# Two transformer blocks on one core: window-attention logits computed two heads at a time, and another order of work between the mixer and the experts

## The reference, cut to what matters

```
# first block: sliding-window attention, 8 query heads on 2 key/value heads, with sinks
s = einsum(q, k) * 64**-0.5 + bias            # per head: 64-wide dot products, 128-query blocks, 256-key band
p = softmax(concat([masked s, sink]))[..., :-1];  o = p @ v
# second block, behind the mixer
x  = x + merged @ w_out
h2 = x * rsqrt(mean(x*x) + eps) * norm2_g
g_logits = h2 @ w_router_group + b_rg;   e_logits = h2 @ w_router_expert[group] + b_re
group = argmax(g_logits);   two best experts of the 8 in the group, softmax over the two
y = sum over the two of  gate * ((silu(h2 @ w_gate[e]) * (h2 @ w_up[e])) @ w_down[e])
out = rmsnorm(x + y)
```

## Time and profile before

| | us |
|---|---|
| median of 3 runs | 730.55 (730.4 to 730.85) |
| the profiled execution's own time | 730.1 |
| its span, from the first to the last instruction | 728.2 |
| TensorE busy | 670.5 (92%) |
| VectorE busy | 333.3 (46%) |
| ScalarE busy | 302.5 (42%) |
| GpSimd busy | 78.5 (11%) |

### The profile page before, as it was taken

One profiled execution on the slowest core, in us unless ns is written; L12 is line 12 of the kernel. 1 busy time (PEld: TensorE's weight loads), 2 busy tenths in 40 slices (PEclk: granted clock), 3 DMA queues, 4 the chain that ended last, 5 costly groups with the idle time before them and its releaser, 6 DMA issues.

```text
span 728.2 us, 11450 instructions
## 1 busy us (share of the span) xinstructions
PE 670.5 (92%) x4599; PEld 514.4 (71%) x4599; DVE 333.3 (46%) x576; ACT 302.5 (42%) x512; POOL 78.5 (11%) x58
## 2 busy tenths in 40 slices
PE   6999999899999999998999999998999996768774
PEld 5887865699999999976988999975644442323222
DVE  3145442755566666577553564666632221212113
ACT  3235353554554454455563453334333332222223
POOL 0000000132333333321013000000000000000000
PEclk9999999999999999999999999999999999999998
DMA  8942133354554555542443349557899999999994
GB/s 343 424 181 85 58 116 116 119 190 164 194 201 173 177 194 200 180 174 79 154 174 116 116 174 365 213 198 318 357 422 422 419 422 421 421 421 420 421 421 203
DMA packets 25390, 181.41 MB, mean 249 GB/s; under 512 B 2816, under 2 KB 3072, under 8 KB 3840
## 3 DMA queue, kind: packets, MB, share of 16 engines
q1 hardware_dynamic: 25200, 180.69, 63.8%
q10 hardware_dynamic: 144, 0.07, 0.1%
HBM read 179.70 MB, written 1.05 MB: 248 GB/s over the span
## 4 chain that ended last, share of the span: by engine, by line
PE 71%; DMA 16%; DVE 7%; ACT 4%; issue 1%; POOL 1%; ACTq 0%; SPq 0%; DVEq 0%; POOLq 0%
PE psum L910 39%; DMA more_units<-units_in 7%; PE psum L603 4%; PE psum L1147 4%; DMA early_unit<-units_in 4%; DMA X<-units_in 4%; PE psum L701 3%; PE psum L1171 3%; PE psum L611 3%; PE psum L1163 3%; PE psum L1154 2%; DVE ffn_w_low L474 2%; PE psum L660 2%; ACT ffn_w_high L469 1%; DVE arena L2029 1%
## 5 line engine op out<-in xcount | busy, mean ns | idle before, releaser
L474 DVE TENSOR_TENSOR ffn_w_low<-ring,ffn_w_high 128x2048 fp32r<-128x2048 f32 x57 | 134.6, 2362 | 119.1 <-ACT ffn_w_high L469 119.0
L469 ACT ACTIVATE ffn_w_high<-ring 128x2048 fp32r<-128x2048 f32 x56 | 107.2, 1914 | 144.1 <-PE psum L910 143.8
L910 PE MATMUL psum<-ht_high,ffn_w_high 128*128 128x256 f32 x576 | 163.8, 284 | 1.8 <-DVE ffn_w_low L474 1.1
L910 PE MATMUL psum<-ht_low,ffn_w_high 128*128 128x256 f32 x576 | 163.0, 283 | 0.0
L910 PE MATMUL psum<-ht_high,ffn_w_low 128*128 128x256 f32 x576 | 163.0, 283 | 0.0
L910 PEld LDWEIGHTS psum<-ht_high,ffn_w_high 128*128 128x128 f32 x576 | 110.5, 192 | 3.5 <-issue 1.6
L910 PEld LDWEIGHTS psum<-ht_low,ffn_w_high 128*128 128x128 f32 x576 | 110.5, 192 | 0.3
L910 PEld LDWEIGHTS psum<-ht_high,ffn_w_low 128*128 128x128 f32 x576 | 110.5, 192 | 0.0
L2342 DVE SCALAR_TENSOR_TENSOR weighted<-psum,arena,weighted 128x512 fp32r<-128x512 f32 x31 | 23.3, 751 | 119.4 <-ACT weighted L1669 119.4
L1365 ACT ACTIVATE arena<-psum 128x512 f32<-128x512 f32 (+6 forms) x65 | 34.5, 538 | 87.5 <-PE psum L1147 64.7
L1751 POOL TENSOR_TENSOR rstd<-ms,neghalf 128x1 f32<-128x1 f32 (+3 forms) x19 | 13.3, 698 | 480.1 <-DVE ms L1805 342.0
(11 more groups left out here) (346 smaller groups left out, 1022.1 us busy)
## 6 DMA issues: line engine op xcount, KB each, us to landing
ring<-units_in SPq DMA_DIRECT2D x99, 1024.0 KB, 4.8
more_units<-units_in SPq DMA_DIRECT2D x34, 1024.0 KB, 26.3
small_units<-units_in SPq DMA_DIRECT2D x10, 1024.0 KB, 25.5
early_unit<-units_in SPq DMA_DIRECT2D x5, 1024.0 KB, 26.2
HN<-units_in SPq DMA_DIRECT2D x5, 1024.0 KB, 26.5
features_unit<-units_in SPq DMA_DIRECT2D x4, 1024.0 KB, 24.6
X<-units_in SPq DMA_DIRECT2D x4, 1024.0 KB, 25.0
rows<-units_in SPq DMA_DIRECT2D x4, 1024.0 KB, 26.0
```

Source lines behind the costliest of these rows:

```text
L469: nc.scalar.activation(parts_slot(n)[0], w, ACT.Copy).then_inc(hi_ready, 1)
L474: nc.vector.tensor_tensor(l, ring[:, n % RING, :], h.bitcast(fp32), SUB).then_inc(lo_ready, 1)
L910: last = mm(o, l[a], r[b], start=start and (a, b) == pairs[0], stop=stop and (a, b) == pairs[-1])
```

## The change

Each window-attention call of `logits` for s = 0 to 7 is replaced: four calls of `paired_logits` compute two heads each, one on partitions 0 to 63 into bank 0, one on 64 to 127 into bank 1, alternating. The head order, and with it the side of the key and value heads, is s % 2. The calls that stood for the second head of each pair are gone.

Behind the mixer: the last `w_out` unit goes bank by bank, with `half_done` after banks 5 and 6; token half 1 is added to X in two halves; transposes 4 to 7 of token half 1 wait for the second of them. ScalarE sums the squares of token half 1 after its copies of the transposes. `LT` is copied by VectorE. The low parts of both token halves are made by quarters of 256 features, the first after the selection, the other three between the two halves of `PGR`. The gather waits for them quarter by quarter and token half by token half. Group 2's copy stands ahead of the tables (L2277 to L2282). The first `stay_busy` has two products instead of four.

```
-SWA_ORDER = [0, 1, 4, 5, 2, 3, 6, 7]
+SWA_ORDER = [0, 4, 1, 5, 2, 6, 3, 7]
 sync:
-                    sp.wait_ge(hn_lo, 3)
+                    sp.wait_ge(hn_lo, 8)
 tensor:
+            def paired_logits(pair):
+                if pair > 0:
+                    pe.wait_ge(s_read, 2 * pair)
+                for qb in range(TT):
+                    nk = P * (qb + 1)
+                    for b in range(2):
+                        last = mm(psum[:, b, qb * P:qb * P + nk], QA[b * HD:(b + 1) * HD, pair, qb * P:(qb + 1) * P],
+                                  KA[b * HD:(b + 1) * HD, 0:nk], start=True, stop=True)
+                        if qb == TT - 1:
+                            last.then_inc(s_done, 1)
             token_quarter(6, w, 0) ...
-            logits(0)
+            paired_logits(0)
             token_quarter(6, w, 1)
-            logits(1)
...
             turn(0)
-            logits(2)
+            paired_logits(1)
...
-            logits(3)
...
-            logits(4)
+            paired_logits(2)
             token_quarter(5, w, 1)
-            logits(5)
...
             turn(4)
-            logits(6)
+            paired_logits(3)
...
             turn(5)
-            logits(7)
...
-                for kk, tt in BY_TOKENS if j == 3 else BY_ROWS: ...
+                for kk, tt, n in BY_BANKS if j == 3 else [...]: ...
+                    if j == 3 and kk == 1 and (tt, n) in ((0, 1), (1, 0)):
                         last.then_inc(half_done, 1)
...
-            stay_busy(4, 2, c_("iota"))
+            stay_busy(2, 2, c_("iota"))
...
-            pe.wait_ge(hn_lo, 2)
             for g in range(8):
...
                 for bank, m, slots in gathered(g):
                     for tt in range(TT):
+                        if g % 4 == 0:
+                            pe.wait_ge(pg_ready, g // 2 + tt + 1)
+                        if g < 4:
+                            pe.wait_ge(hn_lo, 2 * g + tt + 1)
 scalar:
-            mean_squares(10, [X[:, tt, :] for tt in range(TT)], 7)
+            mean_squares(10, [X[:, 0, :]], 7)
             take_transposes(4, None)
+            (wait for X and) nc.scalar.activation(junk, X[:, 1, :], ACT.Square, ...)   # then HNH 0, HNH 1
-            act.wait_ge(lg_done, 1)
-            copy(LT, psum[:, 0, 0:S]).then_inc(logits_sb, 1)
 vector:
             dve.wait_ge(half_done, 5)
-            add_mixed(0)
+            tt_op(X[:, 0, :], ...)
+            dve.wait_ge(half_done, 6)
+            tt_op(X[:, 1, 0:LEFT], ..., psum[:, 6, :], ADD).then_inc(x_ready, 1)
             add_eps_of(10, 0)
             dve.wait_ge(unit_used, U_EXP)
-            add_mixed(1)
-            add_eps_of(10, 1)
+            tt_op(X[:, 1, LEFT:], ..., psum[:, 7, :], ADD).then_inc(x_ready, 1)
             take_transposes(4, None)
...
-            stt(HNL[:, 0, :], ...).then_inc(hn_lo, 1)
+            dve.wait_ge(lg_done, 1)
+            V_.tensor_copy(LT, psum[:, 0, 0:S]).then_inc(logits_sb, 1)
+            add_eps_of(10, 1)
             dve.wait_ge(lg_done, 2)
...
             dve.wait_ge(hn_hi, 2)
-            stt(HNL[:, 1, 0:LEFT], ...)
+            low_parts(0)                      # two instructions of 128x256
...
                 if half == 0:
-                    stt(HNL[:, 1, LEFT:], ...)
+                    for quarter in range(1, 4):
+                        low_parts(quarter)    # six instructions of 128x256
...
+            take_gathered(2)
             (the tables: for a, (oh, rank, weight) in ...)
-            take_gathered(2)
             take_gathered(5)
             take_gathered(6)
```

More of the change, by code:

```diff
@@ L578, in transposes @@
                         pe.wait_ge(x_ready, 7 + tt)
+                        late = 2 if tt == 1 else None
                     else:
+                        late = None
                         pe.wait_ge(hn_dve, (2 * stage + 2 if stage else 1) + tt)
@@ L584, in transposes @@
                     for b in range(KD // 2):
+                        if b == late:
+                            pe.wait_ge(x_ready, 9)
                         for k in range(2):
@@ L651, in logits @@
                     q_at = slice(qb * P, (qb + 1) * P)
[L652 to L655, removed]
+                    if s < SWA_HEADS + MLA_HEADS:
                         l, r = QMT[0:MLA_QK, s - SWA_HEADS, q_at], KMT[0:MLA_QK, s - SWA_HEADS, 0:nk]
@@ L678, in values @@
                 if s < SWA_HEADS:
-                    v = [VA[:, tt, HD * (s % 4 // 2):HD * (s % 4 // 2) + HD] for tt in range(TT)]
+                    v = [VA[:, tt, HD * (s % 2):HD * (s % 2) + HD] for tt in range(TT)]
                 elif s < SWA_HEADS + MLA_HEADS:
@@ L1079, in _ @@
                 w = parts(U_WOUT2 + j)
[L1080 to L1086, removed]
+                for kk, tt, n in BY_BANKS if j == 3 else [(kk, tt, n) for kk, tt in BY_ROWS for n in range(2)]:
+                    a = kk * D + n * 512
+                    last = by_parts(psum[:, 4 + 2 * tt + n, :],
+                                    [v[:, 2 * j + kk, tt * P:(tt + 1) * P] for v in (HTH, HTL)],
+                                    [v[:, a:a + 512] for v in w], j == 0 and kk == 0, j == 3 and kk == 1)
+                    if j == 3 and kk == 1 and (tt, n) in ((0, 1), (1, 0)):
                         last.then_inc(half_done, 1)
@@ L1286, in mean_squares @@
             def mean_squares(event, parts, ready=None, dump=junk):
-                assert len(parts) == NORM_PARTS[event]
+                assert len(parts) <= NORM_PARTS[event]
                 at = D
@@ L1614, in _ @@
             split_hi(act, U_WOUT2 + 3)
-            mean_squares(10, [X[:, tt, :] for tt in range(TT)], 7)
+            mean_squares(10, [X[:, 0, :]], 7)
             take_transposes(4, None)
+            act.wait_ge(x_ready, 9)
+            act.wait_ge(squares_summed, parts_before(10) + 1)
+            nc.scalar.activation(junk[:, :], X[:, 1, :], ACT.Square, scale=D ** -0.5, accum_out=ms[:, 10, 1:2]
+                                 ).then_inc(squares_summed, 1)
             for tt in range(TT):
@@ L2190, in _ @@
                 split_lo(dve, U_WOUT2 + n)
-            def add_mixed(tt):
-                tt_op(X[:, tt, :], X[:, tt, :], psum[:, 4 + 2 * tt:6 + 2 * tt, :].rearrange("p a b -> p (a b)"), ADD
-                      ).then_inc(x_ready, 1)
             dve.wait_ge(half_done, 5)
-            add_mixed(0)
+            tt_op(X[:, 0, :], X[:, 0, :], psum[:, 4:6, :].rearrange("p a b -> p (a b)"), ADD).then_inc(x_ready, 1)
+            dve.wait_ge(half_done, 6)
+            tt_op(X[:, 1, 0:LEFT], X[:, 1, 0:LEFT], psum[:, 6, :], ADD).then_inc(x_ready, 1)
             add_eps_of(10, 0)
             dve.wait_ge(unit_used, U_EXP)
-            add_mixed(1)
-            add_eps_of(10, 1)
+            tt_op(X[:, 1, LEFT:], X[:, 1, LEFT:], psum[:, 7, :], ADD).then_inc(x_ready, 1)
             take_transposes(4, None)
@@ L2205, in _, with low_parts @@
             V_.memset(XS[:, :, SLOTS:], 0.0).then_inc(pad_zero, 1)
-            dve.wait_ge(hn_hi, 1)
-            stt(HNL[:, 0, :], X[:, 0, :], rstd[:, 10, 0:1], HNH[:, 0, :].bitcast(fp32), MUL, SUB).then_inc(hn_lo, 1)
+            dve.wait_ge(lg_done, 1)
+            V_.tensor_copy(LT, psum[:, 0, 0:S]).then_inc(logits_sb, 1)
+            add_eps_of(10, 1)
             dve.wait_ge(lg_done, 2)
             roots_ready(10)
+            def low_parts(quarter):
+                at = slice(quarter * 2 * P, (quarter + 1) * 2 * P)
+                for tt in range(TT):
+                    stt(HNL[:, tt, at], X[:, tt, at], rstd[:, 10, tt:tt + 1], HNH[:, tt, at].bitcast(fp32), MUL, SUB
+                        ).then_inc(hn_lo, 1)
             for tt in range(TT):
@@ L2244, in _ @@
             dve.wait_ge(hn_hi, 2)
-            stt(HNL[:, 1, 0:LEFT], X[:, 1, 0:LEFT], rstd[:, 10, 1:2], HNH[:, 1, 0:LEFT].bitcast(fp32), MUL, SUB).then_inc(hn_lo, 1)
+            low_parts(0)
             dve.wait_ge(rank_done, 1)
@@ L2262, in _ @@
                 if half == 0:
-                    stt(HNL[:, 1, LEFT:], X[:, 1, LEFT:], rstd[:, 10, 1:2], HNH[:, 1, LEFT:].bitcast(fp32), MUL, SUB).then_inc(hn_lo, 1)
+                    for quarter in range(1, 4):
+                        low_parts(quarter)
             step.mark(V_.tensor_copy(RN, ranks))
@@ L2274, in _, with take_gathered @@
             step(tt_op(w2, w1, ex, MUL))
+            def take_gathered(g):
+                dve.wait_ge(xs_done, g + 1)
+                for bank, m, slots in gathered(g):
+                    last = ts_op(XS[:, m, slots], bank, v_("norm2", m), None, MUL)
+                last.then_inc(xs_dve, 1)
+            take_gathered(2)
             for a, (oh, rank, weight) in enumerate(((OH1, r1, w1), (OH2, r2, w2))):
```

1 line of the change is left out of this document (removed).

## The result

| | before | after |
|---|---|---|
| median, us | 730.42 (6 runs, 730.19 to 730.85) | 724.37 (6 runs, 724.23 to 724.9) |
| the profiled execution's own time, its span | 730.1, 728.2 | 724.38, 722.5 |

The ratio is 0.9918, with a 95% interval of 0.9906 to 0.9931: 6.0 us less, where 6.3 were forecast (the time itself, 724.3, is within 0.1). The two executions profiled differ by 5.7.

A forecast was written before the change was run, and what follows sets the result against it. The end was taken to be bound by TensorE's mixer end, then the DMA stream of expert weights. 4.2 us in front plus 2.1 behind gave 6.3: 730.1 to 723.8, median 724.3, range 723.5 to 727.2 at 8 in 10.

The forecast's parts named there:

- What bounds the kernel: Whole kernel: the end is tied to when TensorE ends the mixer (495.99) and how long DMA is empty behind it.
- the hole: DMA stream of expert weights ahead of unit 19: 2.5 us at 66 GB/s, holding 2.1 us of idle time.
- The front, 4 x 1.04 = 4.2 us: Window heads' logits: four calls go, each worth 0.85 us plus 0.19 for the projection behind it.
- side by side: Paired calls: the two 64-partition halves run at once, so a pair lasts as long as one call; saving 4.2 us.
- the other end: Paired calls: halves run one after the other, second head adds 0.65 us, saving only 1.6 us; chance 0.06.
- rival 4: Window heads: VectorE and ScalarE become late, front gain 0.3, total 728.1; nearest wait has 0.7 us cover; chance 0.05.
- The steps behind the mixer: Router to gather: selection 1.75 us earlier, one 1.4 us wait at group 3, group 7 ending 518.4 instead of 521.0.
- The cap, 2.1 us: Behind the mixer: only the hole can be won, 2.1 us, if unit 19 goes out by about 518.9, against 521.11.
- the ramp: Ramp of the hole in the DMA stream: 0.3 us, counted only in the range's low end as saved too.
- 1 us from issue to flow: Unit 19: data flows 1 us after issue; with the skill's 2 us, 0.6 us of the hole would stay.
- Rival 3: Experts' stage: a half-clock stretch of TensorE falls on its last 3 us and doubles them, 727.3; chance 0.08.
- The sum: Whole kernel: 4.2 + 2.1 = 6.3 us less, giving 723.8 for the profiled execution and 724.3 for the median.

The follow-up runs named there:

- e1: The kernel before with the paired calls alone, everything behind the mixer as before: 726.68 us, ratio 0.9941.
- e4: The kernel after, but the issue of unit 19 and all units behind it waits until TensorE has used two units of the experts: 725.95 us, ratio 0.9934.
- e9: The kernel after, but both matmuls of a paired call read q and k from partitions 0 to 63: 727.18 us, ratio 0.9953.
- e3: The kernel after, with each paired call's matmuls on partitions 0 to 63 listed first, then those on 64 to 127: 724.43 us, ratio 0.9910.
- e2: The kernel before with the part behind the mixer alone, head logits one by one as before: 728.74 us, ratio 0.9969.
- e5: The kernel after, with VectorE's three copies of ranks, counts and starts moved ahead of the six low parts: 723.89 us, ratio 0.9906.
- e8: The kernel after, with group 2's copy out of PSUM behind the tables again: 726.29 us, ratio 0.9934.
- e6: The kernel after, with weight units 10 and 11 sent ahead of the mixer's end into two free slots: 723.96 us, ratio 0.9905.
- e11: The kernel after with units 10 and 11 early, the rank, count and start copies ahead, and token half 0's low parts on GpSimd: 725.87 us, ratio 0.9937.

## Why the prediction was right

- **What bounds the kernel.** Two things set the end, the mixer's end and the hole. e1 moves only the first, e4 only the second, and the time follows each.
- **The front, 4 x 1.04 = 4.2 us.** 4.28 at the mixer's end, of which 0.09 lies ahead of the first call, in how the two executions start; 4.16 in e1's trace counted the same way, and 4.0 in its median. The choice of "side by side" was right, and e9 gives the price of the other end, 0.64 us a pair for the 0.65 worked out. The reason given was only half: the earlier trace rows showed halves listed in turn, and I took the turn for the condition. e3 shows that it isn't, at least over four passes.
- **The heads' other engines (rival 4).** No wait of TensorE in the stretch: the 0.7 us of cover held.
- **The steps behind the mixer.** The selection was to start 1.75 earlier; 1.43 were measured (5.03 for 6.46 us behind the mixer's end), the step of this chain that was mis-sized most: TensorE starts the router at 493.56, 1.85 behind the mixer's end, where 1.5 was worked out for the copies of the transposes. The ranks' idle 0.70 went. First gather forecast at about 505, came at 505.03; one wait at group 3, 1.3 for 1.4; none at group 6; unit 19 at 514.60 for 514.3. Counted from the mixer's end that is 0.38 us late, all of the 0.4 that the prediction had in reserve.
- **The cap, 2.1 us: right by luck.** 1.86 came at the last landing in the trace, 1.85 in e2's. But two errors cancel in this term. The stretch from 512 to 526 us shows them, in the kernel before, the one after and e5:

```profile
512.00:526.00 14.00, 12.58 (x104) 10.13 (x107) 8.74 (x38) 5.64 (x14) 0.00 (x0) 1.00 0.86 337
512.00:526.00 14.00, 13.20 (x112) 7.27 (x112) 5.61 (x23) 5.35 (x14) 0.00 (x0) 1.00 1.00 400
512.00:526.00 14.00, 12.16 (x103) 6.19 (x104) 5.63 (x24) 4.91 (x13) 0.00 (x0) 1.00 1.01 420
```

Of 421 GB/s in full flow, the kernel before lacks 14 x (421 - 337)/421 = 2.8 us, the one after 0.7 and e5 nothing. So the hole was worth 2.8 and not 2.1 (2.4 at the last landing, by e5), since the ramp behind it (274 GB/s from 522 to 524) was left out of the sum and put at only 0.3 in the range. And it did not close as forecast: unit 19 was to be out by 518.9 in the old clock, it went out at 514.60 + 4.28 = 518.88, and 0.7 us stayed open. What was won is 2.8 - 0.7.
- **1 us from issue to flow: too short.** The first data do come about 1 us behind the issue, but the flow is not full then. Four us from the issue of unit 19 in the kernel before:

```profile
521.11:525.11 4.00, 3.75 (x32) 2.17 (x32) 0.23 (x1) 1.75 (x4) 0.00 (x0) 1.00 0.78 258
```

That is 4 x (421 - 258)/421 = 1.5 us of full flow missing, and by this estimate unit 19 has to be out that much ahead of the time at which the engines run dry. In e5, where it goes out 1.1 us earlier than in the kernel after, nothing is missing. The prediction set the 2.0 us of the Trainium skill, "DMA: Bandwidth & Descriptors", section "Anatomy of one DMA", against its 1 us: 0.6 of the hole would then stay. 0.7 of the flow did stay, and the trace's 1.5 us lies between the two figures. That is no measurement of the 2.0: the section gives it for GpSimd's DMAs and puts most of it behind the last byte, which is not what is read here.
- **Rival 3, in small.** A stretch of 0.50 ended at 704.9, 6 us ahead of the last unit's landing. It did not double the last work, but left TensorE 0.4 behind. Where these stretches fall differs from kernel to kernel (e2 has one of 10.2 us at 683.0 and loses nothing). e3, which is the kernel after but for the order inside the four calls, has none behind 682.7 until its last unit has landed, and its down product begins 0.04 behind the landing. So this 0.4 does not come with the change as such; what places the stretches is open.
- **The sum.** 6.3 forecast, 6.0 in the medians, 5.7 in the profiled executions: 0.1 more in the front, 0.24 less behind the mixer, 0.48 lost in the tail. Against the medians that is within what the intervals leave open. The time itself came out closer than the gain, since the median of the kernel before is 0.1 below the 730.55 that the prediction started from.

## What to carry to other kernels

Ahead of a stretch that the DMA engines bound, ask for one number: when does the load go out behind which the stream never stops again. What moves it late moves the end by nearly as much (e4, e8), loads put ahead of it do next to nothing (e6), and once it is early enough to fill the ramp there is no more to win (e5). Count the ramp: here 1.5 us of full flow is missing behind an issue on idle engines, not only the 1 us to the first data. Two 64-row products that fit beside each other cost one, so pair them where their results can both be kept; and before work is moved from VectorE to GpSimd, count what runs on VectorE at that time.

## What the hardware showed that was not expected

- Products on the two 64-partition halves overlap also when one half's four passes are listed behind the other's four (13 ns apart in e3). The prediction had thought of alternation as the condition.
- GpSimd subtractions of 128x256 (four in 2.78 us) go with VectorE's 128x8 two-tensor operations taking 0.65 us each instead of 0.17, almost four times, and leave its reductions at 0.16 (e11).
- On idle DMA engines the first data come 1 us behind the issue, but 1.5 us of full flow is missing over the first four (before).
